# The adaLN products of a 4-layer kernel move from TensorE to GpSimd (32 blocks, one Trainium2 core)

## What is computed

```
c_act = jax.nn.silu(c)                       # 1024 numbers
for l in range(2):
    mod = c_act @ ada_w[l] + ada_b[l]        # 1024 x 6144, float32
    sh1, sc1, gt1, sh2, sc2, gt2 = split(mod, 6)
    h = rms_norm(x, norm1_g[l]) * (1.0 + sc1) + sh1
    ...
```

## Time and profile before

| what | value |
| --- | --- |
| median of 3 runs | 1851.52 us |
| all three runs | 1850.48, 1851.52, 1865.01 us |
| span of the profiled execution | 1848.6 us |
| TensorE (PE) busy | 1789.5 us, 97% |
| VectorE (DVE) busy | 1291.4 us, 70% |
| ScalarE (ACT) busy | 1014.5 us, 55% |
| GpSimd (POOL) busy | 29.5 us, 2% |
| DMA, mean | 182 GB/s |

### The profile page before, as it was taken

One profiled execution on the slowest core, in us unless ns is written; L12 is line 12 of the kernel. 1 busy time (PEld: TensorE's weight loads), 2 busy tenths in 40 slices (PEclk: granted clock), 3 DMA queues, 4 the chain that ended last, 5 costly groups with the idle time before them and its releaser, 6 DMA issues. The chain is left out here.

```text
span 1848.6 us, 37836 instructions
## 1 busy us (share of the span) xinstructions
PE 1789.5 (97%) x15229; PEld 1660.0 (90%) x15229; DVE 1291.4 (70%) x1997; ACT 1014.5 (55%) x1582; POOL 29.5 (2%) x48
## 2 busy tenths in 40 slices
PE   7999999999999899999999999999998999999999
PEld 7996788889889698998989999989998999998999
DVE  6848777676777987777777767665556875676555
ACT  6645565555576765555556654454445565455443
POOL 0000000000000000000000001000000000100000
PEclk9999999999999999999999999999999999999999
DMA  8540566766775566566634430445553442044553
GB/s 325 182 159 1 195 227 242 269 254 257 263 278 181 218 236 241 216 217 253 249 112 174 144 115 3 161 159 185 202 183 133 140 160 92 12 173 160 184 203 114
DMA packets 44897, 336.17 MB, mean 182 GB/s; under 512 B 4976, under 2 KB 5232, under 8 KB 6768
## 3 DMA queue, kind: packets, MB, share of 16 engines
q1 hardware_dynamic: 38736, 277.89, 41.5%
q0 software_dynamic: 4608, 50.33, 7.2%
q10 hardware_dynamic: 1440, 6.33, 0.9%
HBM read 333.48 MB, written 1.05 MB: 181 GB/s over the span
## 5 line engine op out<-in xcount | busy, mean ns | idle before, releaser
L686 DVE TENSOR_TENSOR w_lo<-raw,w_hi 128x1024 fp32r<-128x1024 f32 x526 | 639.3, 1224 | 379.5 <-ACT w_hi L677 369.5
L677 ACT ACTIVATE w_hi<-raw 128x1024 fp32r<-128x1024 f32 x526 | 555.0, 1060 | 589.9 <-PE unit L708 375.6
L706 PE MATMUL unit<-h_hi,w_hi 128*128 128x256 f32 x2656 | 751.0, 283 | 23.6 <-DVE h_lo L2124 8.0
L707 PE MATMUL unit<-h_lo,w_hi 128*128 128x256 f32 x2656 | 742.7, 280 | 0.0
L708 PE MATMUL unit<-h_hi,w_lo 128*128 128x256 f32 x2656 | 742.4, 280 | 0.0
L706 PEld LDWEIGHTS unit<-h_hi,w_hi 128*128 128x128 f32 x2656 | 503.3, 190 | 35.4 <-issue 22.6
L708 PEld LDWEIGHTS unit<-h_hi,w_lo 128*128 128x128 f32 x2656 | 505.4, 190 | 0.0
L707 PEld LDWEIGHTS unit<-h_lo,w_hi 128*128 128x128 f32 x2656 | 503.2, 189 | 1.3
L706 PE MATMUL acc<-mv_hi,w_hi 128*128 128x256 f32 x640 | 177.1, 277 | 0.0
L707 PE MATMUL acc<-mv_lo,w_hi 128*128 128x256 f32 x640 | 177.1, 277 | 0.0
L708 PE MATMUL acc<-mv_hi,w_lo 128*128 128x256 f32 x640 | 177.1, 277 | 0.0
(11 more groups left out here) (415 smaller groups left out, 1982.9 us busy)
## 6 DMA issues: line engine op xcount, KB each, us to landing
raw<-w_in SPq DMA_DIRECT2D x263, 1024.0 KB, 4.8
ada_ring<-ada_in POOLq DMA_DIRECT2D x32, 1536.0 KB, 7.6
h<-rows_in ACTq DMA_DIRECT2D x5, 512.0 KB, 4.8
keep<-gates_in ACTq DMA_DIRECT2D x1, 1280.0 KB, 10.1
par<-par_in ACTq DMA_DIRECT2D x1, 1036.0 KB, 10.9
x<-x_in SPq DMA_DIRECT2D x2, 512.0 KB, 4.9
out<-x SPq DMA_DIRECT2D x4, 256.0 KB, 2.3
con<-con_in ACTq DMA_DIRECT2D x1, 950.0 KB, 18.0
```

What stands on the lines that cost most here:

```text
L677: act(half(w_hi, c, k), raw[c % RAW][:, CW // 2 * k:CW // 2 * (k + 1)], ACT.Copy).then_inc(S("high_parts"), 1)
L686: tt(half(w_lo, c, k), raw[c % RAW][:, CW // 2 * k:CW // 2 * (k + 1)], half(w_hi, c, k).bitcast(f32), ALU.subtract).then_inc(S("chunk_spli ...
L706: mm(out, w, m, start=first, stop=False)
L707: mm(out, w, ml, start=False, stop=False)
```

## The change

GpSimd now multiplies each block, in its slot, by `cact` (two instructions of four row tiles), and adds the eight row tiles in a tree (4, 2, 1) down to one tile of 384 columns. VectorE transposes this tile from SBUF in blocks of 32 x 32 and sums each group of 32 columns by a `tensor_reduce`, in place of the copy. All 32 `pe_ada` on TensorE go, with their waits; `pe_mod` stays. A slot is free for the next load when VectorE's transpose has read it (`ada_turned`) and no longer when TensorE's matmuls are done. GpSimd works block by block; where the next block lies in the other slot its load is issued ahead of the present block's products. Some semaphores of the first stage are joined into `dt_act_steps`, with values that follow.

```diff
-        def pool_ada(pool):
-            for n in range(2 * ADA_N):
-                    pool.wait_ge(S("ada_rows"), before + 1)
-                ada_load(pool, s, n)
+        def pool_ada(pool, link):
+            def load(n):
+                s = SLOT[n]
+                if TURN[n] > 1:
+                    before = max(m for m in range(n) if SLOT[m] == s)
+                    pool.wait_ge(S("ada_turned"), before + 1)
+                ada_load(pool, s, n)
+            def weigh(n):
+                tiles = ada_slot[SLOT[n]]
+                pool.wait_ge(S(f"ada_loaded{SLOT[n]}"), 16 * TURN[n])
+                for a in (0, 4):
+                    by = cact[:, a:a + 4].unsqueeze(2).to_broadcast([P, 4, ADA_W])
+                    ins = nc.gpsimd.tensor_tensor(tiles[:, a:a + 4, :], tiles[:, a:a + 4, :], by, ALU.mult)
+                link(ins)
+                for k in (4, 2):
+                    link(nc.gpsimd.tensor_tensor(tiles[:, 0:k, :], tiles[:, 0:k, :], tiles[:, k:2 * k, :], ALU.add))
+                nc.gpsimd.tensor_tensor(tiles[:, 0, :], tiles[:, 0, :], tiles[:, 1, :], ALU.add
+                                        ).then_inc(S("ada_summed"), 1)
+            load(0)
+            load(1)
+            pool.wait_ge(S("dt_act_steps"), 3)
+            weigh(0)
+            for n in range(1, 2 * ADA_N):
+                both = n > 1 and n + 1 < 2 * ADA_N and SLOT[n + 1] != SLOT[n]
+                if both:
+                    load(n + 1)
+                weigh(n)
+                if not both and n + 1 < 2 * ADA_N:
+                    load(n + 1)
-        def pe_ada(pe, n, bank, i=None, per=2):
...
-        def dve_ada(dve, n, bank, i=None, per=2):
+        def dve_ada_summed(dve, n, i=None, per=2):
-            dve.wait_ge(S("ada_rows"), at(i, per, n + 1))
+            dve.wait_ge(S("ada_summed"), at(i, per, n + 1))
-            nc.vector.transpose(ada_turned[:, :], bank[:, 0:ADA_W]).then_inc(S("ada_turned"), 1)
+            nc.vector.transpose(ada_turned[:, :], ada_slot[SLOT[n]][:, 0, :]).then_inc(S("ada_turned"), 1)
-            nc.vector.tensor_copy(dst, ada_turned[:, :].rearrange("p (a b) -> p a b", b=32)[:, :, 0]
-                                  ).then_inc(S("ada_cols"), 1)
+            nc.vector.tensor_reduce(dst, ada_turned[:, :].rearrange("p (a b) -> p a b", b=32), AX.X, ALU.add
+                                    ).then_inc(S("ada_cols"), 1)
```

More of the change, by code:

```diff
@@ L996, in softplus @@
                 link(act(r_b, r_b, ACT.Ln, bias=one("one", HR)))
-                act(r_one[:, 0:1], pr("a_log", 0, HR), ACT.Exp).then_inc(S("dt_log"), 1)
+                act(r_one[:, 0:1], pr("a_log", 0, HR), ACT.Exp).then_inc(S("dt_act_steps"), 1)
             def row_decays():
@@ L1002, in row_decays @@
                 act(r_ncs, r_cs, ACT.Copy, scale=-1.0)
-                act(r_a, r_cs, ACT.Exp).then_inc(S("dt_decays"), 1)
+                act(r_a, r_cs, ACT.Exp).then_inc(S("dt_act_steps"), 1)
             def last_tap(j):
@@ L1025, in act_ssd @@
             ac.wait_ge(S("par_loaded"), 32)
-            act(cact[:, :], par[:, PAR["c"]:PAR["c"] + 8], ACT.Silu).then_inc(S("c_act"), 1)
+            act(cact[:, :], par[:, PAR["c"]:PAR["c"] + 8], ACT.Silu).then_inc(S("dt_act_steps"), 1)
             silu(0)
@@ L1040, in act_ssd @@
             act(neg_up_r[:, :], cn("neg_up"), ACT.Copy)
-            act(cs_parts[:, :], misc[1][:, 256:384], ACT.Copy).then_inc(S("dt_decays"), 1)
+            act(cs_parts[:, :], misc[1][:, 256:384], ACT.Copy).then_inc(S("dt_act_steps"), 1)
             for n in range(8):
@@ L1679, in dve_lru @@
                     square_gap(q + 3)
[L1680 to L1681 removed]
+            dve_ada_summed(dve, 18)
+            dve_ada_summed(dve, 19)
         def ada_load(pool, s, block):
@@ L1697, in pool_ada @@
                     before = max(m for m in range(n) if SLOT[m] == s)
-                    pool.wait_ge(S("ada_rows"), before + 1)
+                    pool.wait_ge(S("ada_turned"), before + 1)
                 ada_load(pool, s, n)
-        def pe_ada(pe, n, bank, i=None, per=2):
-            s = SLOT[n]
-            pe.wait_ge(S(f"ada_loaded{s}"), at(i, 16, 16 * TURN[n]))
-            if i is not None:
-                pe.wait_ge(S("ada_turned"), at(i, per, n - per + 1))
-            for k in range(8):
-                g = 32 * (k % 4)
-                ins = mm(bank[g:g + 32, 0:ADA_W], cact[:, k:k + 1].to_broadcast([P, 32]),
-                         ada_slot[s][:, k, :], start=(k < 4), stop=(k >= 4))
-            ins.then_inc(S("ada_rows"), 1)
@@ L1727, in build @@
         GAP = {"ffn0": 0, "lru": 16, "ffn1": 20, "in2": 30}
         def pe_gap(pe, stage, second, name, n0):
-            n = GAP[second]
-            if n == 0:
-                pe.wait_ge(S("c_act"), 1)
-            x_updated(pe, stage)(0)
-            pe_ada(pe, n, accb[0])
-            pe_ada(pe, n + 1, accb[1])
-            if n == 20:
+            if GAP[second] == 20:
                 pe.wait_ge(S("mod_done"), 1)
```

42 lines of the change are left out of this document (11 added, 31 removed).

## The result

The changed kernel takes 2083.4 us in the median of four runs (2080.5 to 2092.4), the kernel before 1851.0 beside it: 1.125 times as long, interval 1.121 to 1.129. The forecast was 1963 us, with a range from 1858 to 1988: slower, as said, by 232 us where 111 were said. The direction and the mechanism (the two engines take turns on SBUF) held; the size did not.

A forecast was written before the change was run, and what follows sets the result against it. TensorE was taken to bound both FFNs, with VectorE next. Stalls 38.4, first FFN 49, second FFN -3, first stage 8, blocks 16, 18, 20 15, reduce 2 and clock 2 gave 111 us: 1851.5 + 111 = 1963, range 1858 to 1988.

The forecast's parts named there:

- The price of a block on GpSimd: GpSimd's products and sums for one block: 11.9 us, in proportion to a 512-element row; 8.4 to 12.8 as bounds.
- The three stalls: VectorE stands still before the second transpose at blocks 17, 19 and 21: 38.4 us in all.
- TensorE's relief: The 22 blocks inside the FFNs each free TensorE for 1.43 us: 31.5 us; nothing for the other ten.
- The far end for the ports: GpSimd and VectorE on SBUF: each waits for the other's whole instruction; forecast case, 1963 us, chance 0.60.
- the first rival: No SBUF contention between GpSimd and VectorE: full relief, three stalls stay, +11 us, 1862 us; chance 0.22.
- The step that failed: First FFN: VectorE loses 8.7 us a block, a pair takes 22.0 us, 13 periods cost 49 us.
- The hand-worked order: In a pair, GpSimd's five instructions meet a split, the low part, half a tap group, a split, a tap group.
- The upper bound of that term: First FFN, 13 periods: 90 us if VectorE's 13.3 and GpSimd's 11.9 us did not overlap at all.
- The forecast's own range: Range of the serial-ports case: 1925 to 1995 us, its upper end half way to the terms' upper ends.
- The second FFN: One block in two pairs: 34.3 us against 34.86; 7 periods and the start give -3 us (-10 to 6).
- done ahead: Blocks 30 and 31 add no stall, since load 31 waits for block 29 only.
- The clock (2 us): Added TensorE idling at gaps and perhaps the stalls lowers its granted clock: 2 us (0 to 8).

The follow-up runs named there:

- The run with memsets: Against the changed kernel, GpSimd's arithmetic is replaced by writing zeros: eight memsets of 1536 columns and one of 384 a block; 1863.7 us, ratio 1.007.

## Why the prediction was wrong

*Held.* The price of a block on GpSimd: 11.9 us alone, as said, though by two errors that cancel: a product of 1536 takes 2.73 us (5.46 for two), less than the 3.1 in proportion, and a sum of 1536 without a broadcast 3.43, more. That the sum came out was luck. The three stalls: 37.6 us for 38.4. TensorE's relief: 20.1 us for blocks 2 to 15 in the run with memsets, for 18.6. The far end for the ports: whole instructions in turn, with the times above. The Trainium skill (SBUF — State Buffer, Who interferes with whom) states it for a VectorE instruction of two SBUF inputs against a GpSimd instruction that reads SBUF. The traces agree: the split waits beside products, sums and copies (6.76, 3.77 and 2.73 us for 1.23), not beside memsets (1.228 at most). The same section of the Trainium skill counts `tensor_scalar` among the VectorE instructions that can enter a mode with two ports, and so contend; here the one of ten columns took 5.90 us for 0.17. The run with memsets lands on the first rival, 1863.7 for 1862, so that this rival's reason (no contention) is the only part of it that fell.

*The step that failed* is VectorE's side of a pair: "VectorE loses 3.0 + 3.0 + 1.1 + 1.6 + 0 = 8.7 us a block", "a pair takes 22.0 us" and with them "13 x (22.0 - 18.24) = 49 us". In the loop a pair takes 25.0 us (the transposes of blocks 2 and 13 are at 309.4 and 584.3, 11 pairs apart), and these two windows, before and after, ten pairs each, say of what. Before:

```profile
310.00:492.00 182.00, 182.00 (x1359) 160.55 (x1357) 127.39 (x190) 93.08 (x130) 5.29 (x10) 1.00 0.70 259
```

After:

```profile
334.00:584.00 250.00, 187.12 (x1203) 170.47 (x1202) 231.58 (x192) 94.27 (x130) 143.49 (x60) 0.86 0.51 189
```

DVE is busy for 12.7 us a pair before and 23.2 after: its own work with the reduce is 13.1 (13.3 said), the loss 10.0 (8.7 said), and it stands still for 1.8 (0 said). The measured 91.2 is 13 x (24.46 - 17.44); between it and 49 lie 42 us:
- 13 x 1.34 = 17.4 us of loss. The first split waits for two products, 5.5 us where one was counted (3.0). The hand-worked order had one split ahead of the low part; a chunk has two halves, and there are two (at 386.03 and 392.72 above). So the sums meet the second split and the low part, not taps, and the overlap with the taps was taken where the order did not give it.
- 13 x 1.84 = 23.9 us of VectorE standing still. 1.0 us a pair of it are waits for ScalarE's `w_hi` (4.5 before), 0.5 waits for its own taps, as before. In the pair shown, the held splits delay the low part, PE stands for 6.45 us until it is there, ScalarE's last half of the pair waits 1.69 us for PE's matmuls, and VectorE 0.86 us for ScalarE. A sum of VectorE's busy times alone has no such waits.
- 10.4 us in the period before: 18.24 us holds for the loop, but the last two of the 13 are 13.7 and 12.5 us long, and the mean is 17.44.
- Less 9.7 us: the last two periods after are 21.4 and 21.5 us in place of 25.0 (7.1), and VectorE's own work was taken 0.2 too high (2.6).

The waits of that pair on PE, ACT and DVE:

```profile
399.50 0.79 PE L706 MATMUL acc<-w_hi,mv_hi 128*128 128x512 f32 x1 [6.45 <-DVE mv_lo L791]
```

```profile
407.09 1.06 ACT L677 ACTIVATE w_hi<-raw 128x1024 fp32r<-128x1024 f32 x1 [1.69 <-PE acc L708]
```

```profile
408.19 1.23 DVE L686 TENSOR_TENSOR w_lo<-raw,w_hi 128x1024 fp32r<-128x1024 f32 x1 [0.86 <-ACT w_hi L677]
```

The upper bound of that term, "if nothing overlapped (13.3 + 11.9), 90", is near what came, but by other parts, so by luck: VectorE loses 1.9 us less than the block's 11.9, and stands still for 1.8. The forecast's own range ended half way to it and should have given it more weight.

*The second FFN* was to gain 3 us. In its loop two pairs took 34.9 us and take 37.0, where "13.3 + 12.3 + 8.7 = 34.3" was said. The same window view (897 to 1082, five times two pairs) has DVE busy for 33.5 us of the 37.0; before it was 24.8. So own work 25.2 and loss 8.3 are no more than said (25.6 and 8.7), and the step that failed is again the time in which VectorE stands still, 3.5 us where none was counted; 1.8 of it are waits for ScalarE's `w_hi`. The sum over two pairs takes it that VectorE is busy in both. That one pair is held by VectorE and the other waits as before is read from this, not tested. The 15.4 us from 21 to 22 (1 was said) are blocks 22 and 23: GpSimd makes them one after the other (products at 838.8 and 852.4), both beside the head of the stage.

*Not costed:* blocks 30 and 31 were counted as "done ahead", which they are, but the 28 us of GpSimd's work for both lie in the last pair beside the splits: 17.8 us from 29 to 30. The other places outside the loops (first stage 17.8 for 8; blocks 16, 18 and 20 34.2 for 15) say the same: a block there costs 9 to 13 us, about VectorE's whole loss or more, and half of that or less was taken. The clock (2 us) can't be told apart: it fell to 0.86 in the first FFN, but there PE waits for VectorE anyway.

## What to carry over

Work that is moved to an idle engine is not free when that engine shares SBUF with the one that is next in line: here a GpSimd instruction that read SBUF held the VectorE instruction of two SBUF operands that met it until it was done, and the 1.4 to 1.8 us of TensorE a block were bought with 10 of VectorE. As a first price of such a move take the sum of both engines' work (25.2 us a pair here, 25.0 measured; one case, and its parts did not come out one by one), and take an overlap off only where the other engine's operands lie elsewhere. Smaller GpSimd instructions cost VectorE less (6.3 us a block for 10.3), but then see who waits: GpSimd became the bound. Before looking to the idle engine, look at the gaps of the busy ones: VectorE's waits for ScalarE took 14 of the 32 blocks at some 6 us each, as long as the work came in pieces no longer than a wait.

## What the runs showed of the hardware that was not expected

- Two GpSimd products that follow a load's issue directly run as one for VectorE: 5.46 us at 18 places of 18. With one linked write of a column (0.12 us) between issue and products, or the load behind them, a split gets in after the first; the kernel is 47 and 32 us faster. In 17 of the 18 places VectorE's instruction had started, by its record, 0.1 to 0.4 us before the first product, and still waited for both. The cause is open.
- A small instruction can pay as much as a large one: a product of 10 columns (0.17 us) took 5.90 us beside the two products.
- A GpSimd write (memset of 1536 columns, 1.39 us) doesn't hold a split (1.228 us at most), a GpSimd copy does (2.73).
- Taps whose source is in PSUM kept their 0.47 us in every kernel, though one operand and the output lie in SBUF.
